# Conv-branch variance per token column, VectorE scaling from PSUM, and the group-norm gain folded into the output weights

## The reference, cut to what matters

```python
def head_group_mixer(h, positions, w_in, conv_w, conv_b, conv_ln_w, conv_ln_b, ret_gn_w, w_out):
    proj = h @ w_in
    ca, cb, rq, rk, rv, rg = jnp.split(proj, cuts, axis=-1)
    y_conv = conv_module(ca, cb, conv_w, conv_b, conv_ln_w, conv_ln_b)
    y = retention(rq, rk, rv, positions)          # rotary on q and k, 8 heads of 64 columns
    mu = jnp.mean(y, axis=-1, keepdims=True)
    var = jnp.mean(jnp.square(y - mu), axis=-1, keepdims=True)
    y = (y - mu) * lax.rsqrt(var + EPS) * ret_gn_w.reshape(RET_HEADS, RET_DV)
    y_ret = jax.nn.silu(rg) * y.reshape(B, S, RET_HEADS * RET_DV)
    return jnp.concatenate([y_conv, y_ret], axis=-1) @ w_out

def conv_module(a, b, conv_w, conv_b, ln_w, ln_b):
    y = depthwise_conv31(a * jax.nn.sigmoid(b), conv_w) + conv_b
    mu = jnp.mean(y, axis=-1, keepdims=True)      # over the 512 conv channels of one token
    var = jnp.mean(jnp.square(y - mu), axis=-1, keepdims=True)
    return jax.nn.silu((y - mu) * lax.rsqrt(var + EPS) * ln_w + ln_b)
```

## Time and profile before

| | |
|---|---|
| median of 3 runs | 2469.12 us (2458.54 to 2470.46) |
| the profiled execution | 2463.76 us, of which the span of the profile is 2462.2 us |
| mean granted clock of TensorE | 0.99 of full speed |
| busy share of the span | PE 97%, DVE 71%, ACT 46%, POOL 9% |

### The profile page before, as it was taken

How to read it: one execution, slowest core, us unless ns; L and a number is a source line. 1 busy time by engine, 2 the same in 40 slices (tenths; PEclk the granted TensorE clock), 3 DMA queues, 4 the chain that set the end, 5 groups by cost and what they waited for, 6 DMA issues and landing times.

```text
span 2462.2 us, 31226 instructions
## 1 busy us (share of the span) xinstructions
PE 2395.3 (97%) x11980; PEld 1967.7 (80%) x11980; DVE 1752.0 (71%) x2188; ACT 1140.0 (46%) x1631; POOL 226.2 (9%) x232
## 2 busy tenths in 40 slices
PE   9999899999999999999999999999999999999996
PEld 7878788889888878888888898766786888888884
DVE  7999834324348986786676943577358999999987
ACT  4324624424243343333334420466154877777765
POOL 1000710000000011001100100000113211101100
PEclk9999999999999999999999999999998999999998
DMA  4111221301113224223321410100248999999996
GB/s 157 69 43 35 73 98 43 138 34 44 35 52 100 81 86 137 103 69 102 128 103 35 153 62 18 52 18 18 94 164 330 365 383 386 403 395 393 395 386 238
DMA packets 116319, 370.28 MB, mean 150 GB/s; under 512 B 6309, under 2 KB 15701, under 8 KB 116208
## 3 DMA queue, kind: packets, MB, share of 16 engines
q1 hardware_dynamic: 94832, 293.63, 31.4%
q0 software_dynamic: 21376, 75.12, 9.5%
HBM read 343.50 MB, written 25.26 MB: 150 GB/s over the span
## 4 chain that ended last, share of the span: by engine, by line
PE 83%; DVE 11%; issue 2%; ACT 2%; DMA 1%; POOLq 0%; SPq 0%; POOL 0%; DVEq 0%; ACTq 0%
PE banks L469 20%; PE banks L471 20%; PE banks L470 20%; DVE conv_out L1733 4%; PE banks L2859 4%; PE banks L2861 4%; PE banks L2860 4%; PE banks L3062 1%; PE banks L578 1%; PE banks L2802 1%; PE banks L2769 1%; DVE expert_w_lo L2422 1%; PE banks L3029 1%; DVE w_lo L463 1%; PE banks L2995 1%
## 5 line engine op out<-in xcount | busy, mean ns | idle before, releaser
L2422 DVE TENSOR_TENSOR expert_w_lo<-expert_w,expert_w_hi 128x2048 fp32r<-128x2048 f32 x189 | 426.9, 2287 | 28.9 <-ACT expert_w_hi L1566 27.5
L1566 ACT ACTIVATE expert_w_hi<-expert_w 128x2048 fp32r<-128x2048 f32 x192 | 366.6, 1918 | 153.2 <-PE banks L471 128.9
L469 PE MATMUL banks<-act_hi,w_hi 128*128 128x512 f32 x960 | 375.3, 391 | 0.2 <-DVE act_lo L592 0.2
L471 PE MATMUL banks<-act_hi,w_lo 128*128 128x512 f32 x960 | 373.7, 389 | 0.0
L470 PE MATMUL banks<-act_lo,w_hi 128*128 128x512 f32 x960 | 373.6, 389 | 0.0
L469 PE MATMUL banks<-w_hi,act_hi 128*128 128x512 f32 (+1 forms) x640 | 247.0, 386 | 7.5 <-DVE w_lo L463 5.3
L471 PE MATMUL banks<-w_hi,act_lo 128*128 128x512 f32 (+1 forms) x640 | 243.6, 381 | 0.0
L470 PE MATMUL banks<-w_lo,act_hi 128*128 128x512 f32 (+1 forms) x640 | 243.4, 380 | 0.0
L469 PEld LDWEIGHTS banks<-act_hi,w_hi 128*128 128x128 f32 x960 | 180.3, 188 | 38.7 <-issue 1.4
L471 PEld LDWEIGHTS banks<-act_hi,w_lo 128*128 128x128 f32 x960 | 180.2, 188 | 37.8
L470 PEld LDWEIGHTS banks<-act_lo,w_hi 128*128 128x128 f32 x960 | 180.3, 188 | 37.2
(11 more groups left out here) (474 smaller groups left out, 4397.8 us busy)
## 6 DMA issues: line engine op xcount, KB each, us to landing
expert_w<-in_w_gate SPq DMA_DIRECT2D x32, 2048.0 KB, 11.5
expert_w<-in_w_up SPq DMA_DIRECT2D x32, 2048.0 KB, 11.3
expert_w<-in_w_down SPq DMA_DIRECT2D x32, 2048.0 KB, 11.0
ada_w<-in_w_ada POOLq DMA_DIRECT2D x48, 512.0 KB, 4.3
w_raw<-in_mlp_up_w SPq DMA_DIRECT2D x16, 1024.0 KB, 6.0
w_raw<-in_mlp_down_w SPq DMA_DIRECT2D x16, 1024.0 KB, 5.2
w_raw<-in_w_in SPq DMA_DIRECT2D x10, 1024.0 KB, 5.4
w_raw<-in_w_in SPq DMA_DIRECT2D x18, 512.0 KB, 6.1
```

Source lines behind the costliest of these rows:

```text
L469: nc.tensor.matmul(o_, lh, rh, start=start, stop=False)
L471: return nc.tensor.matmul(o_, ll, rh, start=False, stop=stop)
L1566: act.activation(EWH[ring][:, 2 * j:2 * j + 2, :], EW[slot][:, 2 * j:2 * j + 2, :], ACT.Copy).then_inc(w_hi, 1)
L2422: dve.tensor_tensor(EWL[slot][:, c, :], EW[slot][:, c, :], EWH[ring][:, c, :], ALU.subtract).then_inc(w_ready, 1)
```

## The change

- The variance of the conv norm is formed per token column: instead of adding the four channel groups on VectorE and one wide matmul per half, PE makes 16 narrow matmuls per half. Each loads a 128x128 block of the squares as weights and multiplies it by one column of 1/512, so that 128 tokens' variances land on 128 partitions of one PSUM column. The root and the reciprocal are then taken of a 128x8 tile, and PE spreads them back with four 128x128 matmuls per half: the reciprocals of 128 tokens, repeated along the free axis, as weights against the identity.
- VectorE multiplies the centred convolution by these spread reciprocals straight from PSUM, one 128x2048 operation per half, in rounds 3 and 4. GpSimd's eight multiplications go.
- `ret_gn_w` is loaded as one more row of `vector_rows`, transposed with the others, and multiplied into rows 512 to 1023 of the output weights while they are split: two ScalarE copies with a scale per partition, two VectorE operations for the low part, of 128x512 each, in place of one of 128x1024. GpSimd's eight gate multiplications and the load of the broadcast row go.
- The two halves of the angles are worked out together (13 operations in place of 24), and the four rotary products of a tile are two of 128x512 in place of four of 128x256.
- The state of the first round is a copy, so the zeroing of the state goes. The pieces of the output weights are split one round earlier on ScalarE and three rounds earlier on VectorE. ScalarE copies q and k of tile 0 ahead of the two squares, and PE makes the scores of tile 0 directly behind the gate tiles.

```diff
+                if b in (B_WO, B_WO + 1) and half == 1:
+                    for k in (2 * j, 2 * j + 1):
+                        i_ = nc.scalar.activation(WH[:, k, 0:width], raw[:, half, k % 4, 0:width], ACT.Copy, scale=VT[:, k - 4, 37:38])
...
+                if b in (B_WO, B_WO + 1) and j >= 2:
+                    for k in (2 * j, 2 * j + 1):
+                        i_ = nc.vector.scalar_tensor_tensor(out=WL[:, k, 0:width], in0=raw[:, 1, k % 4, 0:width], scalar=VT[:, k - 4, 37:38],
+                                                            in1=WH[:, k, 0:width], op0=ALU.mult, op1=ALU.subtract)
...
+        RSB = BK[5], BK[3]
+        VCB = BK[3]
...
+            pool.dma_start(VEC[37:38, :], ret_gn_w.rearrange("(a n) -> a n", a=1)).then_inc(vec_in, 16)
...
-                    gate_gained(t + 1)
                 if t + 2 < NT - 1:
                     k_decayed(t + 2)
-                if 1 <= t < 5:
-                    ln_scale((t - 1) // 2, (2 * ((t - 1) % 2), 2 * ((t - 1) % 2) + 1))
...
+            def ln_sqrt():
+                act.wait_ge(ln_var, 2)
+                act.activation(SDC[:, :], VCB[:, 0:8], ACT.Sqrt, bias=EPSC[:, 0:1]).then_inc(ln_sd, 1)
...
             for t in range(NT - 1):
                 gate_silu(t)
+            act.wait_ge(ret_in, 32)
+            ret_copy(0)
             ln_square(0)
             ln_square(1)
             gate_silu(NT - 1)
-            act.wait_ge(ret_in, 32)
-            ret_copy(0)
-            ln_sqrt(0)
             ret_copy(1)
-            ln_sqrt(1)
+            split_hi(B_WO, js=(0,))
...
+                if t == 1:
+                    ln_sqrt()
...
+                for n, product in enumerate((by_cos, by_sin)):
+                    i_ = dve.tensor_tensor(product, pairs, CS1[:, n, t, :].unsqueeze(1).to_broadcast([P, 32, 16]), ALU.mult)
...
+            def ln_recip():
+                dve.wait_ge(ln_sd, 1)
+                dve.reciprocal(SDC[:, :], SDC[:, :]).then_inc(ln_sum, 1)
+
+            def ln_scale(h):
+                dve.wait_ge(ln_mean, 2 + h + 1)
+                dve.tensor_tensor(half(YC, h), half(YC, h), RSB[h][:, :].unsqueeze(1).to_broadcast([P, 4, 512]),
+                                  ALU.mult).then_inc(ln_yn, 4)
...
-            for h in range(2):
-                dve.wait_ge(ln_sq, h + 1)
-                add_groups(SQ, h)
             ret_mask(0)
-            ln_recip(0)
             for t in range(NT):
                 if t + 1 < NT:
                     ret_mask(t + 1)
+                    if t == 2:
+                        ln_recip()
                     if t < 3:
-                        ln_recip(t + 1)
-                    elif t < 6:
-                        split_lo(B_WO, js=(t - 3,))
-                    else:
+                        split_lo(B_WO, js=(t,))
+                    elif t in (3, 4):
+                        ln_scale(t - 3)
+                    elif t == 6:
                         ln_low(0)
...
             def ln_var_sum(h):
-                pe.wait_ge(ln_sum, LN0 + h + 3)
-                pe.matmul(LNB[h][:, :], ONESM, SQ[:, 0, h * 512:(h + 1) * 512], start=True, stop=True).then_inc(ln_var, 1)
+                pe.wait_ge(ln_sq, h + 1)
+                for w in range(4 * h, 4 * h + 4):
+                    for c in range(4):
+                        m = pe.matmul(VCB[:, w:w + 1], SQ[:, c, tok(w)], ONESM[:, 0:1], start=(c == 0), stop=(c == 3), skip_group_check=True)
+                m.then_inc(ln_var, 1)
+
+            def ln_rstd_row(h):
+                pe.wait_ge(ln_sum, LN0 + 3)
+                for w in range(4):
+                    m = pe.matmul(RSB[h][:, w * P:(w + 1) * P], SDC[:, 4 * h + w:4 * h + w + 1].to_broadcast([P, P]), IDN,
+                                  start=True, stop=True, skip_group_check=True)
+                m.then_inc(ln_mean, 1)
...
             gemm_tokens(4, T_G, after=before_last_gate)
-            ln_var_sum(0)
             pe.wait_ge(acc_act, freed(T_G + 6)[1])
             ret_scores(0)
             ret_T(1)
-            ln_var_sum(1)
+            pe.wait_ge(acc_act, freed(T_G + 7)[1])
+            ln_var_sum(0)
...
                 ret_sum(t)
+                if t == 0:
+                    ln_var_sum(1)
+                if t in (2, 3):
+                    ln_rstd_row(t - 2)
```

More of the change, by code:

```diff
@@ L723, in build @@
             sem(s) for s in ("ret_y_gated", "ret_sq", "ret_var", "ret_sd", "ret_yn", "ret_ty", "ret_hi", "ret_lo_then_first_rows_lo_half"))
[L724 to L726 removed]
+        ret_in, ret_rs = sem("ret_consts_in"), sem("ret_rstd")
+        ln_mean, ln_d, ln_sq, ln_var, ln_sd, ln_yn, ln_silu, ln_hi, ln_lo = (
+            sem("ln_" + s) for s in ("mean_then_rstd_row_then_hidden_sums", "d_then_w_sums", "sq_then_ada_hi", "var_then_ada_lo", "sd", "yn", "silu", "hi", "lo"))
         x2_in = [sem(f"x_again{t}") for t in range(NT)]
@@ L892, in _ @@
             pool.wait_ge(ret_in, 32)
-            pool.wait_ge(acc_ready, T_G + 8)
+            pool.wait_ge(acc_ready, T_G + 6)
             pool.dma_start(RC[:, :], rconsts[:, RX:RPERS]).then_inc(ret_in, 16)
-            row(GNW[:, :], ret_gn_w, ret_in)
             def k_decayed(t):
@@ new lines, in angles @@
+                a = ANK[:, :, :, :].rearrange("p n t f -> p n (t f)")
+                kk = RT[:, 0:2, 0:128]
+                angle = ANG[:, :, :].rearrange("p t f -> p (t f)")
+                both = angle.unsqueeze(1).to_broadcast([P, 2, 128])
+                dve.tensor_scalar(kk[:, 0, :], angle, float(1 / TWO_PI), 0.25, ALU.mult, ALU.add)
+                dlink(dve.tensor_scalar(kk[:, 1, :], angle, float(1 / TWO_PI), 0.0, ALU.mult, ALU.add))
+                dlink(dve.tensor_scalar(kk, kk, MAGIC, None, ALU.add))
@@ new lines, in angles @@
+                dlink(dve.tensor_scalar(kk, kk, MAGIC, None, ALU.subtract))
+                dlink(dve.scalar_tensor_tensor(out=a, in0=kk, scalar=-c1, in1=both, op0=ALU.mult, op1=ALU.add))
+                dlink(dve.scalar_tensor_tensor(out=a, in0=kk, scalar=-c2, in1=a, op0=ALU.mult, op1=ALU.add))
+                dlink(dve.scalar_tensor_tensor(out=a, in0=kk, scalar=-c3, in1=a, op0=ALU.mult, op1=ALU.add))
+                dlink(dve.tensor_scalar(a[:, 0, :], a[:, 0, :], float(np.pi / 2), None, ALU.add))
@@ L1708, in angles @@
+                dlink(dve.tensor_scalar(kk, a, float(1 / TWO_PI), MAGIC, ALU.mult, ALU.add))
+                dlink(dve.tensor_scalar(kk, kk, MAGIC, None, ALU.subtract))
+                dlink(dve.scalar_tensor_tensor(out=a, in0=kk, scalar=-TWO_PI, in1=a, op0=ALU.mult, op1=ALU.add))
+                dlink(dve.tensor_scalar(a, a, 3.1415925, None, ALU.min))
+                dlink(dve.tensor_scalar(a, a, -3.1415925, None, ALU.max))
                 dve.tensor_copy(POSF[:, 0:1], POS[:, 0:1]).then_inc(trig, 1)
@@ L1835, in ret_state_new @@
                 dve.wait_ge(ret_state, t + 1)
+                if t == 0:
+                    dve.tensor_copy(STATE[:, :, :], KVB[:, :].rearrange("p (g n) -> p g n", g=2)).then_inc(ret_state, 1)
+                    return
                 for g in range(2):
@@ L1860, in ln_center @@
                                   ALU.subtract).then_inc(ln_d, 1)
-            def ln_recip(q):
-                dve.wait_ge(ln_sd, q // 2 + 1)
-                dve.reciprocal(SDL[:, q * 256:(q + 1) * 256], SDL[:, q * 256:(q + 1) * 256]).then_inc(ln_rstd, 1)
+            def ln_recip():
[5 more added lines that the diff above has]
+                                  ALU.mult).then_inc(ln_yn, 4)
             def ln_low(h):
```

85 lines of the change are left out of this document (29 added, 56 removed).

## The result

The changed kernel takes 2472.54 us (median of 19 runs, 2468.04 to 2474.61), the kernel before 2461.84 us (median of 19 runs beside it, 2458.54 to 2471.33). The ratio is 1.0031, with a 95% interval from 1.0021 to 1.0040: 0.3% slower, less than the 0.5% that count as a difference here. It lies inside the range of 2455 to 2475 by the width of that range alone, and outside the likeliest case's own 2461 to 2469. The profiled execution of after took 2472.10 us, of which the span is 2470.5 us, 8.3 us more than before.

A forecast was written before the change was run, and what follows sets the result against it. TensorE (PE), busy 97% of the span, was taken as the bound, so only its idle time or a shorter list could help. 2463.8 - 1.4 + 1.2 + 1.6 = 2465.2 us, range 2455 to 2475.

The forecast's parts named there:

- likeliest case: Whole kernel: the forecast of 2465.2 us itself, with its own range from 2461 to 2469; chance 0.64.
- Term 3: Clock over the narrow sets: one fall expected, 3.2 us at half the pace, +1.6 us; none gives 0, two 3.2.
- sign of being wrong: Retention stage: narrow sets under 2 us, granted clock low over 8 us, or VectorE's PSUM multiplication holding up a state update.
- Rival 3: Retention stage: clock stays at 0.50 from the first narrow set, 29.7 us of PE work doubles, 2493 us; chance 0.05.
- Rival 2: Narrow sets: two or three clock falls, or sets at the lower level, cost 3.2 to 6, 2467 to 2470; chance 0.15.
- Term 2: PE's list from the gate tiles' end to the output of tile 4: 31.3 us against 30.1, +1.2 us.
- Rival 1: Variance matmuls: cheap narrow ones, 0.8 to 0.9 us a half, time 2458.0 us; chance 0.13.
- Term 1: PE's wait at the start of the v tiles: 0.5 + 0.9 us shorter, -1.4 us.
- the seven rotations: Ahead of the v weights on VectorE: two wider products in place of four save 0.9 us over seven rotations.
- the gated half: VectorE, behind the q and k weights' low parts: begins 0.5 us earlier than its 114.65.
- The covers: Retention rounds: VectorE's added work fits under PE's, 5.3 under 5.5 us with a spread, 4.3 under 4.66 in rounds 0 to 2.

## Why the prediction was wrong, step by step

**Term 3 failed, by its size.** "I expect one such fall, priced as the one at the v wait: 3.2 us at half the pace", +1.6 us. The mechanism was right, narrow matmuls under a fully busy PE do lower the clock, but the fall was 20.5 us long and cost 40.81 - 31.34 = 9.5 us. That also meets the prediction's own sign of being wrong, a low clock for more than 8 us. A fall behind a wait, followed by 512-column matmuls, was the wrong model for one that narrow and short matmuls follow. A nearer one stood in the trace of before: the window of the earlier trace rows ends at 1842.0, where I stopped reading, and the fall does not. Taken to its end it reads

```profile
1839.30:1853.00 13.70, 12.38 (x39) 8.79 (x39) 7.54 (x28) 6.07 (x11) 6.83 (x7) 0.50 1.01 394
```

with transpositions, a second narrow set and one wait of 1.32 us in it. Priced at 13.7 us, the same term would have been +6.9 and the forecast 2470.5. Rival 3 named what happened, "the mix of narrow and short matmuls holds the clock at 0.50", but gave it the whole stage or nothing, and 0.05; the argument against it, that the same rounds ran at 0.97 before, says nothing about rounds that begin with the clock down. Rival 2 gave the size up to 6 us and stopped short.

**Term 2 was right.** 31.3 us were worked out for the list; 31.34 were measured where the clock stays up. The price of a set, 3.7 us from the router's 0.116 a record, was 3.58 with 128 columns and an estimated 6.79 / 2 = 3.4 with one. Rival 1 falls with it.

The Trainium skill, "TensorE: Matmul & The Clock Gate", section "Wait — 56ns, not 53.3ns?", gives 25 ns as the least time between the starts of small matmuls, an estimated 0.8 us for the 32 records of a set. With a 128x128 weight load to each record a set took 3.58 us here, so that least time was not the price. The same page of the Trainium skill, section "What's actually happening", ties the clock to how busy PE has been. If busy is read from the profile's busy time, 20.50 of 20.50 busy us at 0.51 disagree.

**Term 1 was right in one half.** The wait of the v tiles fell by 0.9 us, the seven rotations:

```profile
159.50 0.47 PE L479 MATMUL banks<-w_hi,act_hi 128*128 128x512 f32 x1 [3.93 <-DVE w_lo L473]
```

The clock fell behind it as before (0.53 from 160.3 to 163.7 us). The 0.5 us of the gated half did not come: the 2.1 us saved on the angles were used up long before, by a wait for PE and one for ScalarE, as VectorE's timeline shows:

```profile
46.88 0.69 DVE L1719 TENSOR_TENSOR conv_in<-banks,conv_out 128x512 f32<-128x512 f32 x1 [0.96 <-PE banks L481]
...
65.64 1.23 DVE L473 TENSOR_TENSOR w_lo<-w_raw,w_hi 128x1024 fp32r<-128x1024 f32 x1 [1.23 <-ACT w_hi L460]
```

I had looked for such a limit at the q and k weights only, 45 us later.

**The covers held.** VectorE's part of rounds 3 and 4 in the changed kernel:

```profile
286.62 2.28 DVE L1870 TENSOR_TENSOR conv_out<-conv_out,banks 128x2048 f32<-128x2048 f32 x1
288.82 0.87 DVE L1839 SCALAR_TENSOR_TENSOR ret_state<-ret_state,ret_columns,banks 128x256 f32<-128x256 f32 x2
```

The state of round 3 ends at 289.69, and PE comes to the next keys at 290.90, without idle time; a round with a spread takes 292.23 - 286.63 = 5.60 us, 5.5 were worked out. The low parts in rounds 0 to 2 take 1.22, 1.22 and 1.37 us, and no low part stalls beside GpSimd. The projection did not begin within 3 us of before, but 8.6 us later, by Term 3 and the tail's clock.

With the measured terms the sum is 2463.8 - 0.9 + 1.3 + 9.5 - 1.5 (the tail) = 2472.2 us; measured 2472.1. These terms are read from the same executions, so the sum shows that none is missing and tests nothing further.

## What to carry to other kernels

Read the granted clock of every stretch beside its busy time, and follow a low stretch to its end before you price one like it; a PE that is busy all the time can be at half its pace. Here a record with a new 128x128 fp32 weight took 0.11 us with one column and with 128, and the 128 kept the clock up; no run has a width between the router's 16, where it fell, and 128. Read the mean clock of every execution before you compare medians: one profiled execution may be of one kind while the median is of another. And when a change bundles parts, price them apart: the small ones carried the gain, the rest took it back.

## What was not expected of the hardware

Eight records of one-column matmuls, 0.95 us, were followed by 13.7 us at 1.2 GHz in the profiled execution, and the same eight with 128 columns by none. Behind two sets together the clock stayed down for 11.4 us of matmuls that run at 2.4 GHz in the kernels with 128 columns. And a wait of 3.23 us had no fall behind it, while one of 3.41 us at the same place in another kernel was followed by 10.2 us at 0.50.
